# A chunked RWKV-7 scan: directions on partition halves, and the state of one chunk beside the inverse of the next

## The reference, cut to what matters

```python
def step(S, inp):
    r_t, w_t, k_t, v_t, kk_t, b_t = inp
    sa = -jnp.einsum("bhvk,bhk->bhv", S, kk_t)
    S = S * w_t[:, :, None, :] + sa[..., None] * b_t[:, :, None, :] + v_t[..., None] * k_t[:, :, None, :]
    return S, jnp.einsum("bhvk,bhk->bhv", S, r_t)

s_fwd_c, y_fwd_c = rwkv_scan(zero_state, fc, 0, reverse=False)
s_bwd_c, y_bwd_c = rwkv_scan(zero_state, fc, 1, reverse=True)
_, y_fwd_x = rwkv_scan(s_fwd_c, fx, 0, reverse=False)
_, y_bwd_x = rwkv_scan(s_bwd_c, fx, 1, reverse=True)
```

## Time and profile before

| | us |
|---|---|
| median of 3 runs (lowest, highest) | 2168.02 (2167.54, 2170.58) |
| the profiled execution | 2174.26 |
| its span, first to last instruction | 2172.5 |
| scan of layer 0, stage to stage | 215.0 to 446.4 |
| scan of layer 1, stage to stage | 1453.0 to 1668.6 |

### The profile page before, as it was taken

How to read it: one execution, slowest core, us unless ns; L and a number is a source line. 1 busy time by engine, 2 the same in 40 slices (tenths; PEclk the granted TensorE clock), 3 DMA queues, 4 the chain that set the end, 5 groups by cost and what they waited for, 6 DMA issues and landing times. The chain is left out here.

```text
span 2172.5 us, 51547 instructions
## 1 busy us (share of the span) xinstructions
PE 1937.1 (89%) x22829; PEld 1559.0 (72%) x22829; DVE 1027.4 (47%) x1713; ACT 751.7 (35%) x1380; POOL 297.9 (14%) x381
## 2 busy tenths in 40 slices
PE   4986888889889999899998998958888889998988
PEld 1671788854568888678886676838787558988988
DVE  1545666562643333443332124566666363545544
ACT  0324333323542222232222113354333453435432
POOL 2102433301100111010001001034331110100000
PEclk8997999999999999999999998979999999999999
DMA  8513000010112323223234851200001114554543
GB/s 322 180 36 145 5 4 5 4 52 22 40 61 68 106 89 97 78 88 107 87 107 178 308 193 57 85 1 5 5 5 44 32 40 150 183 165 155 175 147 126
DMA packets 143452, 203.96 MB, mean 94 GB/s; under 512 B 6718, under 2 KB 123672, under 8 KB 137088
## 3 DMA queue, kind: packets, MB, share of 16 engines
q1 hardware_dynamic: 141728, 198.96, 27.3%
q0 software_dynamic: 1504, 1.71, 0.2%
HBM read 199.61 MB, written 1.05 MB: 92 GB/s over the span
## 5 line engine op out<-in xcount | busy, mean ns | idle before, releaser
L330 DVE TENSOR_TENSOR W_low<-RING,W_high 128x1024 fp32r<-128x1024 f32 x268 | 329.4, 1232 | 461.2 <-ACT W_high L327 460.7
L366 PE MATMUL BANK<-H_high,W_high 128*128 128x512 f32 (+2 forms) x1472 | 511.8, 348 | 19.9 <-ACT H_high L632 9.6
L367 PE MATMUL BANK<-H_low,W_high 128*128 128x512 f32 (+2 forms) x1472 | 507.9, 345 | 0.0
L368 PE MATMUL BANK<-H_high,W_low 128*128 128x512 f32 (+2 forms) x1472 | 507.5, 345 | 0.0
L327 ACT ACTIVATE W_high<-RING 128x1024 fp32r<-128x1024 f32 x268 | 281.1, 1052 | 594.4 <-PE BANK L368 572.2
L366 PEld LDWEIGHTS BANK<-H_high,W_high 128*128 128x128 f32 (+1 forms) x1472 | 279.9, 190 | 65.2 <-issue 27.6
L368 PEld LDWEIGHTS BANK<-H_high,W_low 128*128 128x128 f32 (+1 forms) x1472 | 280.0, 190 | 34.4
L367 PEld LDWEIGHTS BANK<-H_low,W_high 128*128 128x128 f32 (+1 forms) x1472 | 280.1, 190 | 33.9 <-issue 0.6
L1275 PE MATMUL BANK<-RING,WORK 64*64 64x64 f32 x4352 | 162.4, 222 | 14.3 <-issue 8.5
L1275 PEld LDWEIGHTS BANK<-RING,WORK 64*64 64x64 f32 x4352 | 144.6, 134 | 27.1 <-issue 10.4
L366 PE MATMUL BANK<-hidden_high,W_high 128*128 128x512 f32 (+1 forms) x352 | 122.9, 349 | 12.0 <-PEq L2188 12.0
(11 more groups left out here) (307 smaller groups left out, 2825.4 us busy)
## 6 DMA issues: line engine op xcount, KB each, us to landing
RING<-w_in_dram SPq DMA_DIRECT2D x46, 1024.0 KB, 5.5
RING<-w_ffn_in_dram SPq DMA_DIRECT2D x44, 1024.0 KB, 5.1
lation_weights_ffn<-w_mod_dram SPq DMA_DIRECT2D x24, 1024.0 KB, 6.2
RING<-w_ffn_out_dram SPq DMA_DIRECT2D x20, 1024.0 KB, 5.1
tion_weights_opening<-w_mod_dram SPq DMA_DIRECT2D x8, 1024.0 KB, 8.5
ulation_weights_norm<-w_mod_dram SPq DMA_DIRECT2D x8, 1024.0 KB, 6.8
on_weights_features<-w_mod_dram SPq DMA_DIRECT2D x8, 1024.0 KB, 5.0
RING<-w_out_dram SPq DMA_DIRECT2D x8, 1024.0 KB, 5.1
```

Of the source, the lines that this page charges most:

```text
L330: low_ready.mark(nc.vector.tensor_tensor(self.part(1, c), self.raw(c), self.part(0, c).bitcast(FP32), ALU.subtract))
L366: nc.tensor.matmul(out, w[0], x[0], start=start, stop=False)
L367: nc.tensor.matmul(out, w[0], x[1], start=False, stop=False)
L368: return nc.tensor.matmul(out, w[1], x[0], start=False, stop=stop)
```

## The change

`scan` is rewritten and `features` loses `EXCL`.

- **Layout.** For the inverse, direction 0 lies on partitions 0 to 63 and direction 1 on 64 to 127, all 8 heads along the free dimension (`TT_D`, `T_D`, `LT_D`, `LM_D`, `X1_D`, `W_D`; two groups g of four heads each). Masks of both directions are one tile, `[P, LEVELS + 2 * NDIR, HD]` in place of `[P, NDIR, LEVELS + 3, HD]`.
- **Gram.** b and k of a head stand side by side as 128 stationary columns, kk and r as up to 128 moving columns: one matmul a head and direction (16 a step) gives all four Gram matrices on 128 partitions. `BK` is turned by 8 PE transposes of 128x128, v by 8 matmuls against a 128-wide identity.
- **Inverse.** Level products stay 80 x1 matmuls; tx is 80 (T only, with the identity added to x1 on VectorE so that the product is the new T), and the transpose of T comes from VectorE's block transposes. ScalarE copies T out.
- **State and output.** sa and v are stacked on partitions (`SAV`), so a state update is 8 matmuls a direction and an output 16, with all 128 rows. sa and w are kept as before.
- **Pipeline.** The loop runs 9 times; turn i inverts chunk i and, between the inverse's products, does the state and output of chunk i - 1. Buffers that cross turns are doubled. A direction has two exponentials of 64 and 65 columns (`SHRINK`, `GROW`); the subtraction for direction 1 moves from VectorE to GpSimd.

TensorE's order in a turn:

```diff
+                    if inverse:
+                        grams(0)
+                        grams(1)
+                        bk_turn(0)
+                    if s is not None:
+                        w_own()
+                    if inverse:
+                        bk_turn(1)
+                    if s is not None:
+                        w_other()
+                        if need_y:
+                            y_own()
+                    if inverse:
+                        both(x1, 1)
+                    if s is not None:
+                        sa(0)
+                        sa(1)
+                    if inverse:
+                        both(tx, 1)
+                    if need_y:
+                        y_end()
+                    if inverse:
+                        both(x1, 2)
+                    if s is not None:
+                        ds(0)
+                        ds(1)
+                    if inverse:
+                        both(tx, 2)
+                        v_turn()
+                        both(x1, 3)
+                        both(tx, 3)
...
+                        both(x1, 5)
+                        both(tx, 5)
```

Some of its products, with `half(x)` a half of the partitions:

```diff
+                        for j in range(PAIRS):
+                            for h in range(2):
+                                last = mm(BANK[:, 2 * d + h, j * P:j * P + width], BK[d][half(h), j].rearrange("p x t -> p (x t)"),
+                                          QR[d][b][half(h), j].rearrange("p q t -> p (q t)")[:, 0:width], start=True, stop=True)
+                        s_gram[d].mark(last)
...
+                        for h in range(2):
+                            for j in range(PAIRS):
+                                at = (h * PAIRS + j) * HD
+                                last = mm(BANK[half(d), B_SA, at:at + HD], TT_D[c][half(d), h, j], W_D[half(d), h, j], start=True, stop=True)
+                        s_sa[d].mark(last)
...
+                        for j in range(PAIRS):
+                            for h in range(2):
+                                last = mm(BANK[half(h), B_DS[d], j * HD:(j + 1) * HD], BK_TOK[d][c][:, j, h], SAV[d][:, h, j], start=True, stop=True)
+                        s_ds[d].mark(last)
```

VectorE's side of the inverse, and its order in a turn:

```diff
+                        s_first.mark(nc.vector.tensor_tensor(flat(TT_D[b]), flat(LT_D), masks[:, 0].unsqueeze(1).to_broadcast([P, HEADS, HD]), ALU.mult))
+                        dve.wait_ge(*at_step(s_first, i, 1, 1))
+                        s_tt0.mark(nc.vector.tensor_tensor(flat(TT_D[b]), flat(TT_D[b]), eye_heads[:].unsqueeze(1).to_broadcast([P, HEADS, HD]), ALU.add))
...
+                        s_t0.mark(nc.vector.transpose(T_D.rearrange("p g j t -> p (g j t)"), TT_D[b].rearrange("p g j t -> p (g j t)")))
...
+                        s_x1_unit[g].mark(nc.vector.tensor_tensor(X1_D[:, g], quarter(B_X1[g]), eye_heads[:].unsqueeze(1).to_broadcast([P, PAIRS, HD]), ALU.add))
...
+                        s_tt[g].mark(nc.vector.transpose(TT_D[b][:, g].rearrange("p j t -> p (j t)"), T_D[:, g].rearrange("p j t -> p (j t)")))
...
+                        gram_out(0)
+                        begin()
+                        gram_out(1)
+                        x1_with_unit(1, 0)
+                        x1_with_unit(1, 1)
+                        transpose_out(1, 0)
+                        transpose_out(1, 1)
+                    if need_y:
+                        add_y()
...
```

More of the change, by code:

```diff
@@ L120, in shape_constants @@
     stack = lambda m: np.concatenate([m, m], axis=0)
-    masks = []
+    levels, grams = [], []
     for d in range(NDIR):
@@ L131, in shape_constants @@
         incl_t = strict_t | (r == c)
[L133 to L136, removed]
+        levels.append(np.concatenate([-(m.astype(f)) for m in level], axis=1))
+        grams += [stack(strict_t.astype(f)), stack(incl_t.astype(f))]
+    out["masks"] = np.concatenate([np.concatenate(levels, axis=0), *grams], axis=1).astype(f)
     out["eye_heads"] = stack(np.eye(HD)).astype(f)
@@ L1036, in scan, with reads @@
         y0 = 0 if context_y else N
-        def tokens(eng, d, i):
-            return chunk_of(d, i)
         def run(eng, step):
[L1043 to L1047, removed]
+            for i in range(STEPS + 1):
+                step(i, i < STEPS, i - 1 if i > 0 else None, i + 1 < STEPS)
+        def reads(i):
+            return i >= y0
         def at_step(s, i, k=1, n=0):
             return s.sem, s.base + k * i + n
+        half = lambda x: slice(x * HD, (x + 1) * HD)
         first_half = lambda d: slice(HD // 2 * d, HD // 2 * (d + 1))
         later_half = lambda d: first_half(1 - d)
[L1057 to L1062, removed]
+        within = lambda d, part: slice(d * HD + part.start, d * HD + part.stop)
+        B_SA, B_Y, B_DS, B_X1, B_T = 0, 1, (2, 3), (4, 5), (6, 7)
+        gram_banks = lambda d: BANK[:, 2 * d:2 * d + 2].rearrange("p b n -> p (b n)").rearrange("p (g q t) -> p g q t", q=2, t=HD)
+        quarter = lambda bank, a=0: BANK[:, bank, a:a + QUARTER].rearrange("p (j t) -> p j t", j=PAIRS)
+        flat = lambda tile: tile.rearrange("p g j t -> p (g j) t")
         with stage() as block:
@@ L1076, in step @@
+                def step(i, inverse, s, more):
+                    if not inverse:
+                        return
                     for l in range(1, LEVELS):
[L1077 removed]
+                        for g in range(2):
                             if l == 1:
[L1079 to L1082 removed]
@@ L1083, in step @@
-                        if more and l in (3, 5):
-                            d = (l - 3) // 2
-                            operands(i + 1, t[d], d)
+                                for d in range(NDIR):
+                                    pool.wait_ge(*at_step(s_lts[d], i, 1, 1))
+                            pool.wait_ge(*at_step(s_x1[g], i, NL, l - 1))
+                            s_lm[g].mark(nc.gpsimd.tensor_tensor(LM_D[:, g], LT_D[:, g], masks[:, l].unsqueeze(1).to_broadcast([P, PAIRS, HD]), ALU.mult))
@@ L1254, in _ @@
             def _(pe):
-                def each(bank, at, width, lhs, rhs, stride=None):
-                    stride = stride or width
-                    for j in range(PAIRS):
-                        for rows in (UP, DOWN):
-                            last = nc.tensor.matmul(BANK[rows, bank, at + j * stride:at + j * stride + width],
-                                                    lhs(j)[rows], rhs(j)[rows], start=True, stop=True)
-                    return last
-                OWN, OTHER = (UP, DOWN), (DOWN, UP)
```

614 lines of the change are left out of this document (326 added, 288 removed).

## The result

The changed kernel takes 2150.15 us (median of 5 runs, 2148.47 to 2156.42) against 2168.02 for the kernel before (5 runs beside them): a ratio of 0.9914, with a 95% interval of 0.9892 to 0.9936. It is faster, as forecast, but by 17.9 us where 44 had been forecast. The profiled execution has a span of 2146.7 us, that of before 2172.5.

What follows compares the result with a forecast made beforehand. TensorE's instruction supply, with inverse and state in one chain, was taken to bound the scans. Layer 0's -24.3, layer 1's -18.7 and 0.7 elsewhere sum to -43.7 us: median 2168.0 to 2124, range 2060 to 2168.

Steps and rivals of the forecast that it cites:

- The rival of dearer forms: Rival (0.14): block transposes at 1.11, 128-row products one at a time, or full waits between shapes; 26.1 to 28.2 us a turn.
- b: Segment from x1(1) to x1(2), TensorE doing x1, sa, tx and y_end in order: 5.2 us.
- shape changes: Twelve switches of TensorE matmul shape a turn, 0.10 us each, half of them lying in waits: 0.5 us a turn.
- d: Segment of level 3 of the inverse, by its chain of products, additions and copies: 2.7 us.
- e: Segment of level 4 of the inverse, with VectorE doing operands(1) before the additions: 3.4 us.
- segment a: Start of a turn, first Gram matmul to x1(1), VectorE ending last, 0.5 for GpSimd's company included: 5.9 us.
- 0.9 for the clock: Allowance per turn for TensorE partly at 1.2 GHz, from the earlier grants of 0.92 and 0.94: 0.9 us.
- TensorE at 1.2 GHz: Rival (0.12), slower: sparser TensorE work lowers the scans' clock; gain gone at 2.9 us more a turn, mean grant near 0.84.
- f: Segment of level 5 of the inverse, on quarter blocks: 1.9 us.
- c: Segment from x1(2) to x1(3), TensorE doing x1, state, tx and v: 4.2 us.
- the walked chain: Main case (0.50): a scan turn of 24.7 us, between 22.5 and 26.5; 2091 to 2151 us, centre 2124.
- the rival of a shorter chain: Rival (0.18): TensorE groups overlap better, sa 0.5 a direction, no clock loss, cheap transposes and Gram; 21.6 a turn, 2078 us.

Runs made afterwards that it cites:

- The burst: e5 plus 640 independent identity products on TensorE behind the ninth turn of each layer: the burst took 39.5 us, the one execution 2155.83 us.
- e1: Changed kernel with VectorE making the next chunk's operands early, behind x1_with_unit(1, 1), and direction 1's exponentials moved up: 2092.37 us, ratio 0.9633 to the kernel before.
- e3: Changed kernel with GpSimd's masks of levels 4 and 5 cut to one 128x16 corner: 2109.46 us, ratio 0.9714 to the kernel before.
- e2: Changed kernel with identity products filling TensorE's waits behind x1(3) and x1(4): 2133.17 us, ratio 0.9821 to the kernel before.
- e5: e1 with the products of sa taken for both directions in turn, on two array pieces at once: 2082.06 us, ratio 0.9563 to the kernel before.
- e6: e5 with TensorE doing sa before x1(1), and ScalarE's copies reordered to match: 2084.30 us, ratio 0.9579 to the kernel before.
- e7: e1 with the next chunk's Gram products issued in levels 3 and 4, their ScalarE copies behind x1_last: 2091.03 us, ratio 0.9604 to the kernel before.
- e8: Changed kernel with VectorE's operands behind the x1_with_unit passes at levels 3 and 4: 2132.90 us, ratio 0.9799 to the kernel before.

## Why the prediction was right and wrong

**What bounded before: right.** 37 and 34 instruction packets came in the scans after (36 and 34 forecast), one in 5.95 and 6.1 us, so the period no longer sets the time. The burst shows that one in some 4.0 us is what TensorE gets, with 3.92 and 3.85 in before, so the idle time there was read rightly, and the change did remove it. The rule of the Trainium skill (Runtime: NRT & Kernel Launch, "Instruction fetch mechanics") that a crossing is mostly hidden does not hold for this burst, where 1.91 us in 4.00 are not.

**Unit prices: right in the main.** Block transposes 0.445 and 0.711 (0.42 and 0.69 taken), Gram groups 2.06 for two at full clock (2.1), state groups of 16 records 0.54 (0.5). The rival of dearer forms is out. sa is 0.73 a direction, between the value taken (1.0) and its lower bound (0.5), and b came out 0.4 shorter than walked. Four PE transposes took 0.58 (0.43 taken), and the narrow Gram pairs of turns without output, forecast 0.6 shorter, 2.00 in place of 2.06. No run separates the 0.5 taken for shape changes.

**Levels 3 and 4: the step that failed.** "d. Level 3 by its chain ... 2.7" leaves out `operands(0)`, which VectorE's order puts before `x1_with_unit(3)`; "e. Level 4 the same, but VectorE does `operands(1)` (three passes, 1.0) before the additions: 3.4" has them at the price without company. With the passes of 0.94 and GpSimd's masks running beside, d took 3.42 and e 4.49, 1.8 more than forecast for the two. The prediction had the earlier trace rows, with 0.42 going up to 0.99, and charged company only in segment a. e1 and e3 show both halves: 1.5 us of company, 1.6 of place.

**The clock: under-sized, and a consequence.** "0.9 for the clock" took the grant of before, 0.92 and 0.94, as given. The waits of levels 3 and 4, 1.11 and 2.18 us before tx, were new, and after them the clock stood at 0.50 for the Gram products (0.50 to 0.62 in all ten turns with these waits): with level 5, 2.3 us a turn in place of 0.9 (e2: 2.2). The claim that "in a. VectorE ends last" fell with it: TensorE ran from the first Gram product to x1(1) without a gap. The rival "TensorE at 1.2 GHz" named the mechanism, but it put the deciding point at a mean grant near 0.84, and 0.87 took only part of the gain.

**The sum.** Layer 0 came out 13.2 us longer than walked: start 0.7, first turn 2.4, seven turns 11.3, ninth turn -1.2. Six of the seven took about 27.0, and the eighth of the layer, which makes no operands, 22.4. In the turn shown, a and f are 2.3 longer than walked, d and e 1.8, c 0.1, and b 0.4 shorter; 1.4 of that had been set aside for the clock and shape changes, which leaves the 2.3 between 24.7 and 26.97. That the time still falls into the band of the walked chain, 2091 to 2151, is luck: its turns, 22.5 to 26.5, were exceeded, and short last turns made up for some of it. e1 removes both causes, and its segments a, b and c of 6.04, 4.77 and 4.27 are near the walk's 5.9, 5.2 and 4.2; without operands its levels 3 and 4 fall to 2.4 each. The design had the forecast gain in it, and more: 21.6 us a turn is what the rival of a shorter chain had, though only in part for its reasons (nothing lost to the clock, but sa at 0.73 and not 0.5, and operands that cost nothing in their new place). Open is why the same waits left the clock at its upper level in some turns and not in others.

## What to carry to other kernels

When work of the next iteration is slipped into an engine's queue, read which instruction stands behind it and who waits for that one; price it in the company that it will have there, and look for a stretch in which the engine idles anyway. A wait on TensorE costs more than its length if products that set the path follow at half the clock, so a short wait may be worth removing, or filling, for what comes after it. When a reordered version comes out at the busy time of one engine, try less work on that engine first: here that helped (e5), and more overlap did not (e6, e7).

## What was not expected of the hardware

VectorE's passes over two SBUF inputs took 0.41 us alone and 0.94 beside a GpSimd mask, while those of the same size with an input in PSUM never took more than 0.43; where the operands lie went together with whether company cost anything. In a burst TensorE got one packet of 256 instructions in 3.7 to 4.0 us, although it works one off in 2.09 at a clock of 1.00. The clock over the Gram products was low more often the longer TensorE had waited before tx(4), but the same waits did not always give the same clock. After waits of 1.11 and 2.18 us before tx(3) and tx(4) (changed kernel) it was 0.50 to 0.62 in ten turns of ten; after 0.06 and 1.72 (e8) 0.50 to 0.61 in ten of eleven and 1.00 in one; after 0.61 and 1.16 (e3) 0.50 to 0.61 in five and 1.00 in five; after 0.41 and 0.56 (e2) 1.00 in ten of ten.
